# Two groups of gate products together ahead of every second score piece, instead of one ahead of each

## The chip, the cores and the metric

The kernel runs on one core of one Trainium2 chip, in one launch. The time is the device time of one execution in microseconds (us), the median of several executions. A profile is one further execution, recorded engine by engine: TensorE (PE, with its weight loads as PEld), VectorE (DVE), ScalarE (ACT), GpSimd (POOL) and SyncE (SP), which here issues the loads.

## The reference, cut to what matters

Two transformer blocks are computed one after the other on 256 tokens of width 1024. The change touches only the last layer of the second block, a feed-forward layer with 16384 experts (128 x 128), of which each of 8 heads picks 16 per token:

```python
def block(hb):                                   # 128 tokens at a time, TOK_BLOCK = 128
    q = (hb @ w_pq).reshape(TOK_BLOCK, PEER_HEADS, 2, PEER_DHALF)
    s = jnp.einsum('thpd,hpnd->thpn', q, sub_keys).astype(jnp.float32)
    s1, i1 = lax.top_k(s[:, :, 0], PEER_TOPK)
    s2, i2 = lax.top_k(s[:, :, 1], PEER_TOPK)
    ...                                          # idx, top_s: the best 16 of the 256 sums per head
    gate = jax.nn.softmax(top_s, axis=-1).astype(hb.dtype)
    u = expert_u[idx]
    act = jax.nn.gelu(jnp.einsum('thkd,td->thk', u, hb), approximate=False)
    vv = expert_v[idx]
    return jnp.einsum('thk,thkd->td', gate * act, vv)
```

Everything is float32.

## The kernel before, in words

The kernel does not gather experts. It computes the scores of all 16384 experts for all 256 tokens, puts gelu over them, multiplies by a gate that is zero where an expert was not chosen, and multiplies the result with all of `expert_v`. The experts come in 128 pieces of 128. The tile `GE` [128 partitions, 128 pieces, 256 tokens] holds the products of gate and gelu.

A weight piece (512 KB) is loaded by SP into one of 4 buffers `raw`, and is split for TensorE into a high part, which ACT writes (`high`, a copy into the fp32r tile `spl`), and a low part, which DVE writes (`low`, raw minus high, a subtraction of 128x1024). `spl` has 3 places (`NSP = 3`), so `high(i)` waits until TensorE has used piece i-3 (`w_used`). Each program does its part of the split three pieces ahead: `w.past("eu", c)` makes `high(c+3)` on ACT and `low(c+3)` on DVE.

The pieces of `expert_u` (`eu`) run in one loop over c = 0 to 127 that stands once in the program of each engine, in an order written out by hand:

- TensorE (`scores(c)`): 24 matmuls 128x256 in fp32r into one PSUM bank. From c = 47 on, for 64 pieces, `gates(g)` stands ahead of `scores(c)`: 8 matmuls 128x128 in fp16 for the four tokens of group g, from the operands `Ao` and `EB` into another bank. It waits for the one-hots of its group (`Ao`). 4 banks are in turn for both.
- ACT: `put(g)` copies that part of the gates whose pieces have no scores yet from PSUM into `GE`; it waits for DVE's `G_mul` of the same group. Then `scores(c)`: gelu over the bank of the scores, in two parts. Tokens whose gates are already in `GE` (columns 0 to n, n = `gated(c)`) go to the buffer `gl`, the others straight to `GE`. Then `high(c+3)`.
- DVE: `gate_scored(g)` multiplies the gates of group g onto the pieces already scored (a scalar_tensor_tensor that reads PSUM), then `onehots(c+2-GATES)` writes the operands of the group two ahead (two products into `EB`, two into `Ao`), then `gate_chunk(c-1)` multiplies `gl` onto the gates of piece c-1, then `low(c+3)`.
- `EB` and `Ao` have two buffers each (`g % 2`): `onehots(g)` waits until the products of group g-2 are done.

After piece 127 the stage of `expert_v` begins, in which TensorE accumulates the output over 128 pieces of 24 matmuls 128x512.

Below, c is a piece and g a group (before: g = c - 47). E(c) is the moment at which the 24 matmuls of `scores(c)` are issued and TensorE goes on to what stands behind them. All helpers record one line for an operation: L133 is every matmul, L155 every activation, L158 every tensor_tensor, L167 every scalar_tensor_tensor.

Of the kernel before, what the change touches and what calls it, by code (L numbers as in the profile page):

```python
# [23 lines left out]
         ("w_pq", 16, 1024, 1), ("sub_keys", 2, 1024, 0), ("eu", 128, 1024, 1), ("ev", 128, 1024, 1)]  # L24
ON_POOL = ("w_pq", "w_o", "w_xk", "w_xv", "w_rwkv_0", "w_rwkv_1")
EU_POOL, LOOKUP, WO_POOL = 30, 27, 3
CHOICE, GATES, NGRP = 42, 47, 64
PIECES = [(nm, j, n, sp) for nm, cnt, n, sp in ORDER for j in range(cnt)]
AT = {nm: i for i, (nm, j, _, _) in enumerate(PIECES) if j == 0}
SPLIT = [i for i, p in enumerate(PIECES) if p[3]]  # L30
# [186 lines left out]
def bc(ap, axis, n):  # L217
    u = ap.unsqueeze(axis)
    shape = list(u.shape)
    shape[axis] = n  # L220
    return u.to_broadcast(shape)
# [41 lines left out]
def build(nc, T, poff, outs, stop=99):  # L263
# [4 lines left out]
    with ctx:  # L268
# [187 lines left out]

        def gated(c):

            return 4 * min(max(c - GATES + 1, 0), NGRP)

        ge_at = SE.at
        GE = SE("GE", [128, 128, 256])
# [48 lines left out]
        def run(g):  # L511
            for _ in g:
                pass
# [10 lines left out]
        def tensor(pe):  # L524
# [741 lines left out]
            def scores(c):  # L1266
                wh, wl, i = weight("eu", c)
                b = pe.bank("eu", c)
                for k in range(8):
                    cs = slice(k * 128, k * 128 + 128)  # L1270
                    pe.wait_ge("xs_l", k)
                    last = pe.mm3(b[:, 0:256], (wh[:, cs], wl[:, cs]), tuple(t[:, k, :] for t in xT), k == 0, k == 7)
                last.then_inc("w_used", i)
                pe.give("eu", c, "ge", c)

            def gates(g):
                b = pe.bank("gates", g)
                pe.wait_ge("Ao", g)
                for q in range(4):
                    for k in range(2):  # L1280
                        last = pe.mm(b[:, q * 128:q * 128 + 128], EB[:, g % 2, 1, q // 2, :, q % 2], Ao[:, g % 2, k, q // 2, :, q % 2], k == 0, k == 1)
                last.then_inc("gates_ps", g)
                pe.give("gates", g, "G", g)
# [12 lines left out]

            ch = [choose(0), choose(1)]
            for c in range(128):
                if GATES <= c < GATES + NGRP:
                    gates(c - GATES)  # L1300
                scores(c)
                if c == CHOICE + 2:
                    run(ch[0])
                    run(ch[1])
# [21 lines left out]
        def scalar(act):  # L1326
# [374 lines left out]
            def choose(tb):  # L1701
                act.wait_ge("sel_sub", tb)
                act.wait_ge("x5_rs", tb)
                sg_ = sel[:, tb, 2, :].rearrange("p (h k) -> p h k", k=16)
                act.act(sg_, sg_, ACT.Exp, scale=s_x5[tb][1]).then_inc("sel_exp", tb)

            def scores(c):
                n = gated(c)
                if not n:
                    w.past("eu", c)  # L1710
                act.wait_ge("w_used", AT["eu"] + c)
                if n < 256:
                    x = act.act(GE[:, c, n:256], act.ps("eu", c)[:, n:256], ACT.Gelu)
                if n:
                    if c >= GATES + 2:
                        act.wait_ge("W_mul", c - 2)
                    x = act.act(gl[:, c % 2, 0:n], act.ps("eu", c)[:, 0:n], ACT.Gelu)
                x.then_inc("ge", c)
                w.past("eu", c)

            def put(g):

                s = GATES + g
                act.wait_ge("gate")
                act.wait_ge("sel_ps")
                act.wait_ge("G_mul", g)
                act.act(GE[:, s:128, 4 * g:4 * g + 4], act.ps("gates", g)[:, :].rearrange("p (t i) -> p i t", t=4)[:, s:128, :], ACT.Copy, scale=1.0 / GSCALE).then_inc("G", g)
# [5 lines left out]
                act.act(Wr[:, c % 2, 0, :], GE[:, c, :], ACT.Copy).then_inc("W_h", c)  # L1733

            for c in range(128):
                if GATES <= c < GATES + NGRP:
                    put(c - GATES)
                scores(c)
                if c == CHOICE:
                    for tb in range(2):  # L1740
                        choose(tb)
# [11 lines left out]
        def vector(dve):  # L1753
# [116 lines left out]
            for tb in range(2):  # L1870
# [3 lines left out]
                c, s = (bc(trig[:, i, tb, 0:8], 1, 16) for i in (1, 0))  # L1874
# [258 lines left out]
            def directions(j):  # L2133

                js = slice(2 * j, 2 * j + 2)
                z, y, x = be[:, js, :], y_[:, js, :], x2_[:, js, :]
                dve.wait_ge("P")
                dve.tt(ARt[:, js, 1, :], pm[:, js, :], Pc[:, js, :], ALU.mult).then_inc("rho", j)
                yield
                dve.wait_ge("y0", j)  # L2140
                v = dve.tt(z, y, y, ALU.mult).own()
                dve.wait_ge("Pi")
                dve.tt(aa[:, js, :], aa[:, js, :], cum[:, js, :], ALU.mult)
                yield
                dve.after(v)
                dve.after(dve.stt(z, z, -0.5, x, ALU.mult, ALU.mult).own())
                dve.after(dve.stt(y, z, 1.5, y, ALU.add, ALU.mult).own())
                yield
                dve.after(dve.tt(t1[:, js, :], t1[:, js, :], y, ALU.mult).then_inc("kk", j))
                dve.wait_ge("Pp")  # L2150
                dve.tt(ARt[:, js, 0, :], t1[:, js, :], ld[:, js, :], ALU.mult).then_inc("al", j)
                yield
                dve.tt(z, t1[:, js, :], aa[:, js, :], ALU.mult).then_inc("be", j)


            g = directions(0)
# [4 lines left out]
            g = directions(1)  # L2161
# [51 lines left out]
            for tb in range(2):  # L2213
                for i, (sc, half) in enumerate(((1, 0), (0, 1), (1, 1), (0, 0))):
                    g = rows[:, 2048:2240].rearrange("p (j d) -> p j d", j=2)[:, :, 64 + 16 * half:80 + 16 * half]
# [288 lines left out]
            def parted():  # L2504

                dve.wait_ge("slT")
                dve.after(dve.cp(gp[:, 0, :], sg[:, :]).own())
                return dve.tt(gp[:, 1, :], sg[:, :], gp[:, 0, :], ALU.subtract).own()

            def onehots(g):  # L2510
                if g >= 2:
                    dve.wait_ge("gates_ps", g - 2)
                ts = slice(4 * g, 4 * g + 4)
                eb, ao = EB[:, g % 2, :, :, :, :], Ao[:, g % 2, :, :, :, :]
                pair = lambda t, a: bc(t[:, :, 4 * g + 2 * a:4 * g + 2 * a + 2], 2, 128)
                made = [dve.tt(eb[:, :, a, :, :], bc(io2[:, :, :], 1, 2), pair(idx, a), ALU.is_equal).own() for a in range(2)]
                for a in range(2):
                    dve.after(made[a])
                    x = dve.tt(ao[:, :, a, :, :], bc(eb[:, 0, a, :, :], 1, 2), pair(gp, a), ALU.mult)
                x.then_inc("Ao", g)  # L2520

            def gate_scored(g):

                s = GATES + g
                dve.wait_ge("gates_ps", g)
                dve.wait_ge("ge", s - 1)
                o = GE[:, 0:s, 4 * g:4 * g + 4]
                dve.stt(o, dve.ps("gates", g)[:, :].rearrange("p (t i) -> p i t", t=4)[:, 0:s, :], 1.0 / GSCALE, o, ALU.mult, ALU.mult).then_inc("G_mul", g)

            def gate_chunk(c):  # L2530

                n = gated(c)
                dve.wait_ge("ge", c)
                dve.wait_ge("G", n // 4 - 1)
                dve.tt(GE[:, c, 0:n], GE[:, c, 0:n], gl[:, c % 2, 0:n], ALU.mult).then_inc("W_mul", c)
# [11 lines left out]
            for x in ch:  # L2547
                next(x)
            for c in range(128):
                if GATES <= c < GATES + NGRP:  # L2550
                    gate_scored(c - GATES)
                if GATES <= c + 2 < GATES + NGRP:
                    onehots(c + 2 - GATES)
                if c > GATES:
                    gate_chunk(c - 1)
                w.past("eu", c)
                if LOOKUP <= c < CHOICE:
                    next(lk, None)
                if c == CHOICE:
                    for x in ch:  # L2560
                        next(x)
                if c == CHOICE + 2:
                    for x in ch:
                        run(x)
                    dve.after(parted())
# [151 lines left out]

        marks = Marks(nc, ctx)
        lanes = [("pe", tensor), ("dve", vector), ("act", scalar), ("pool", gpsimd), ("sp", sync)]
        for name, program in lanes:  # L2720
            program(Lane(marks, name, ident, banks, {}))
# [11 lines left out]
        @block.tensor  # L2733
        def _(e):
            tensor(lane("pe", e))

        @block.vector
        def _(e):
            vector(lane("dve", e))

        @block.scalar
        def _(e):
            scalar(lane("act", e))
# [81 lines left out]
```

## Time and profile before

| | |
|---|---|
| median of 3 runs | 1484.4 us (1483.9 to 1486.01) |
| the profiled execution | 1486.74 us, its span 1484.7 us |
| granted TensorE clock, mean | 0.995 |
| PE busy | 1441.2 us, 97% of the span |
| DVE busy | 1006.8 us, 68% |
| ACT busy | 721.9 us, 49% |
| pieces with gate products | from 852.8 us to 1065.5 us |

Busy time is an average over stages. What a change inside one loop is worth is read in the time order of that loop: which instruction each engine waits for, and how late it is. Matmuls overlap, so their spacing is read from start to start. A row of the time order that is marked x2 or x24 joins so many instructions of a kind, from the start of the first to the end of the last.

### The profile page before, as it was taken

The page shows a single profiled execution, that of the slowest core. Times are in us where ns is not written, and L with a number is a line of the kernel's source. Part 1 is how long each engine was busy: PE and PEld are TensorE (multiplying, and loading weights), DVE is VectorE, ACT ScalarE, POOL GpSimd, SP SyncE. Part 2 cuts the span into 40 slices and gives each one's busy share as a digit, 9 for nine tenths or more (in the row PEclk, how much of TensorE's full clock was granted, in tenths as well). Part 3 has the DMA queues.
Part 4 walks back from the last instruction along what each step waited for, and adds up shares of the span by engine and source line. Part 5 has one row for each costly group of instructions (what it writes and reads, how often), then busy time and mean ns, then how long its engine had stood idle before and what let it go on. Part 6 is the DMA issues. An engine that isn't in the chain of part 4 may idle for free.

```text
span 1484.7 us, 24608 instructions
## 1 busy us (share of the span) xinstructions
PE 1441.2 (97%) x10160; PEld 1291.4 (87%) x10160; DVE 1006.8 (68%) x1809; ACT 721.9 (49%) x1195; POOL 239.1 (16%) x115
## 2 busy tenths in 40 slices
PE   7999999999998989999999999999999999999998
PEld 6898797998878968979999999999998888888886
DVE  5667465665449787663798788999855555555554
ACT  4565453555344635343544555544444444444443
POOL 0037000000014220539684000000000000000000
PEclk9999999999999999999999999999999999999999
DMA  7634443556552520135566655555565666666663
GB/s 276 217 104 142 144 141 113 157 182 191 190 175 86 167 68 2 45 114 166 175 185 187 182 159 158 156 158 157 162 187 168 190 186 186 190 189 186 186 191 118
DMA packets 64878, 235.23 MB, mean 158 GB/s; under 512 B 7424, under 2 KB 7680, under 8 KB 64512
## 3 DMA queue, kind: packets, MB, share of 16 engines
q1 hardware_dynamic: 63904, 231.60, 50.7%
q10 hardware_dynamic: 864, 2.08, 0.4%
q8 instruction: 80, 1.31, 0.4%
q14 instruction: 30, 0.25, 0.1%
HBM read 232.60 MB, written 1.05 MB: 157 GB/s over the span
## 4 chain that ended last, share of the span: by engine, by line
PE 87%; DVE 9%; ACT 2%; issue 1%; DMA 0%; POOL 0%; DVEq 0%; ACTq 0%; POOLq 0%
PE ps L133 85%; PE ps L142 1%; DVE spl L158 1%; DVE pm L167 1%; ACT QK L155 1%; DVE pm L158 1%; DVE prep L158 0%; DMA hA<-in_x 0%; ACT spl L155 0%; DVE hx L158 0%; DVE pR L158 0%; DVE junk L158 0%; DVE hx L161 0%; DVE be L158 0%; DVE ez L167 0%
## 5 line engine op out<-in xcount | busy, mean ns | idle before, releaser
L133 PE MATMUL ps<-xhl,spl 128*128 128x256 f32 x4944 | 605.8, 283 | 3.5 <-POOL spl L158 1.6
L133 PEld LDWEIGHTS ps<-xhl,spl 128*128 128x128 f32 x4944 | 591.0, 189 | 6.3 <-issue 3.3
L158 DVE TENSOR_TENSOR spl<-raw,spl 128x1024 fp32r<-128x1024 f32 (+2 forms) x356 | 430.3, 1214 | 236.2 <-ACT spl L155 234.6
L155 ACT ACTIVATE spl<-raw 128x1024 fp32r<-128x1024 f32 (+1 forms) x435 | 454.6, 1048 | 273.6 <-PE ps L133 259.0
L133 PE MATMUL ps<-spl,Wr 128*128 128x512 f32 x1536 | 358.7, 395 | 1.1 <-DVE Wr L158 1.1
L133 PEld LDWEIGHTS ps<-spl,Wr 128*128 128x128 f32 x1536 | 288.3, 188 | 71.3 <-DVE Wr L158 1.3
L158 POOL TENSOR_TENSOR spl<-raw,spl 128x1024 fp32r<-128x1024 f32 x79 | 199.8, 2543 | 275.8 <-ACT spl L155 275.3
L155 ACT ACTIVATE Wr<-GE 128x256 fp32r<-128x256 f32 x128 | 53.5, 419 | 183.5 <-PE ps L133 183.5
L158 DVE TENSOR_TENSOR Wr<-GE,Wr 128x256 fp32r<-128x256 f32 x128 | 54.3, 425 | 81.5 <-ACT Wr L155 81.5
L155 ACT ACTIVATE GE<-ps 128x256 f32<-128x256 f32 (+42 forms) x176 | 54.0, 326 | 113.6 <-DVE GE L167 108.4
L133 PE MATMUL ps<-spl,ahl 128*128 128x512 f32 x384 | 90.1, 396 | 0.0
L133 PEld LDWEIGHTS ps<-spl,ahl 128*128 128x128 f32 x384 | 72.2, 188 | 17.6
L133 PE MATMUL ps<-spl,yhl 128*128 128x512 f32 x288 | 69.4, 399 | 1.4 <-ACT vm L155 1.4
L133 PEld LDWEIGHTS ps<-spl,yhl 128*128 128x128 f32 x288 | 53.7, 188 | 14.3 <-ACT vm L155 1.6
L133 PE MATMUL ps<-spl,xhl 128*128 128x512 f32 (+2 forms) x288 | 62.5, 375 | 0.9 <-DVE spl L158 0.8
L133 PEld LDWEIGHTS ps<-spl,xhl 128*128 128x128 f32 x288 | 51.5, 190 | 11.0 <-DVE spl L158 2.0
L158 DVE TENSOR_TENSOR Ao<-EB,gp 128x512 f16<-128x512 f16 x128 | 48.2, 418 | 0.0
L158 DVE TENSOR_TENSOR EB<-io,idx 128x512 f16<-128x512 f16 x128 | 48.0, 417 | 0.0
L133 PE MATMUL ps<-Ao,EB 128*128 128x128 f16 x512 | 40.9, 221 | 0.0
L158 POOL TENSOR_TENSOR stats<-stats,neghalf 128x1 f32<-128x1 f32 (+2 forms) x13 | 8.0, 613 | 202.0 <-DVE stats L161 202.0
L155 ACT ACTIVATE gl<-ps 128x256 f32<-128x256 f32 (+32 forms) x81 | 24.1, 298 | 25.6 <-PE ps L133 25.6
L133 PEld LDWEIGHTS ps<-Ao,EB 128*128 128x128 f16 x512 | 29.7, 97 | 2.7
(341 smaller groups left out, 1156.3 us busy)
## 6 DMA issues: line engine op xcount, KB each, us to landing
raw<-in_eu SPq DMA_DIRECT2D x128, 512.0 KB, 3.6
raw<-in_ev SPq DMA_DIRECT2D x128, 512.0 KB, 4.3
raw<-in_w_up SPq DMA_DIRECT2D x32, 512.0 KB, 3.6
raw<-in_w_down SPq DMA_DIRECT2D x32, 512.0 KB, 4.3
raw<-in_w_in_a SPq DMA_DIRECT2D x16, 512.0 KB, 5.0
raw<-in_w_pq SPq DMA_DIRECT2D x16, 512.0 KB, 3.6
raw<-in_w_rwkv SPq DMA_DIRECT2D x14, 512.0 KB, 3.7
raw<-in_w_in_t SPq DMA_DIRECT2D x8, 512.0 KB, 3.5
```

The source lines that it names most:

```text
L133: return Done(self, self.e and self.e.matmul(out, l, r, start=st, stop=sp))
L142: return Done(self, self.e and self.e.transpose(out, in_, self.ident[0:n, 0:n]))
L155: return Done(self, self.e and self.e.activation(out, a, f, bias=bias, scale=scale, accum_out=acc))
L158: return Done(self, self.e and self.e.tensor_tensor(out, a, b, op))
L167: return Done(self, self.e and self.e.scalar_tensor_tensor(out, a, s, b, o0, o1))
```

## The change

The constant `GATES` goes from 47 to 48. A new helper `groups(c)` gives the groups of a piece: for an even distance from 48 the two groups c-48 and c-47, for an odd one none. TensorE makes both groups' products ahead of `scores(c)`, ACT puts both, DVE does both `gate_scored`, and both count as if they stood at the first piece of the pair. The one-hots stay where they were relative to `GATES`: one group at each piece, `onehots(c + 2 - GATES)`. The even groups thus come one piece later than before, the odd groups at the same piece as before, and all one-hots one piece later. `gated(c)` now goes up by 8 at every second piece. The buffers of `EB` and `Ao` stay at two.

```diff
-CHOICE, GATES, NGRP = 42, 47, 64
+CHOICE, GATES, NGRP = 42, 48, 64
...
         def gated(c):
 
-            return 4 * min(max(c - GATES + 1, 0), NGRP)
+            return 4 * min(max((c - GATES) // 2 * 2 + 2, 0), NGRP)
+
+        def groups(c):
+
+            return range(c - GATES, c - GATES + 2) if GATES <= c < GATES + NGRP and (c - GATES) % 2 == 0 else ()
...
             for c in range(128):
-                if GATES <= c < GATES + NGRP:
-                    gates(c - GATES)
+                for g in groups(c):
+                    gates(g)
                 scores(c)
...
             def put(g):
 
-                s = GATES + g
+                s = GATES + g // 2 * 2
...
-                if GATES <= c < GATES + NGRP:
-                    put(c - GATES)
+                for g in groups(c):
+                    put(g)
...
             def gate_scored(g):
 
-                s = GATES + g
+                s = GATES + g // 2 * 2
...
-                if GATES <= c < GATES + NGRP:
-                    gate_scored(c - GATES)
+                for g in groups(c):
+                    gate_scored(g)
                 if GATES <= c + 2 < GATES + NGRP:
                     onehots(c + 2 - GATES)
```

DVE's order at pieces 102 and 103, before. `GE<-ps,GE` is `gate_scored`, `EB` and `Ao` are the one-hots, `GE<-GE,gl` is `gate_chunk`, `spl<-raw,spl` is `low`; the brackets name the semaphores waited for.

```order
L167 SCALAR_TENSOR_TENSOR GE<-ps,GE 128x102x4 [waits ge,pe_ps]
L158 TENSOR_TENSOR EB<-io_121,idx 128x2x256 x2
L158 TENSOR_TENSOR Ao<-EB,gp 128x2x256 [waits own_dve] x2
L158 TENSOR_TENSOR GE<-GE,gl 128x220 [waits G]
L158 TENSOR_TENSOR spl<-raw,spl 128x1024 [waits w_high]
L167 SCALAR_TENSOR_TENSOR GE<-ps,GE 128x103x4 [waits ge,pe_ps]
L158 TENSOR_TENSOR EB<-io_121,idx 128x2x256 x2
L158 TENSOR_TENSOR Ao<-EB,gp 128x2x256 [waits own_dve] x2
L158 TENSOR_TENSOR GE<-GE,gl 128x224 [waits G]
L158 TENSOR_TENSOR spl<-raw,spl 128x1024 [waits w_high]
```

The same two pieces of DVE in the changed kernel.

```order
L167 SCALAR_TENSOR_TENSOR GE<-ps,GE 128x102x4 [waits ge,pe_ps]
L167 SCALAR_TENSOR_TENSOR GE<-ps,GE 128x102x4 [waits pe_ps]
L158 TENSOR_TENSOR EB<-io_121,idx 128x2x256 x2
L158 TENSOR_TENSOR Ao<-EB,gp 128x2x256 [waits own_dve] x2
L158 TENSOR_TENSOR GE<-GE,gl 128x216
L158 TENSOR_TENSOR spl<-raw,spl 128x1024 [waits w_high]
L158 TENSOR_TENSOR EB<-io_121,idx 128x2x256 x2
L158 TENSOR_TENSOR Ao<-EB,gp 128x2x256 [waits own_dve] x2
L158 TENSOR_TENSOR GE<-GE,gl 128x224 [waits G,ge]
L158 TENSOR_TENSOR spl<-raw,spl 128x1024 [waits w_high]
```

Both `gate_scored` stand at the even piece. The second one-hots stand behind the `low` of the even piece, and nothing but a `gate_chunk` and a `low` is left between them and the next pair.

TensorE's order where the gate products begin, in the changed kernel (`Ao,EB` are gate products, `xhl,spl` scores); before, 8 and 24 matmuls alternated.

```order
L133 MATMUL ps<-xhl,spl 128x256 x72
L133 MATMUL ps<-Ao,EB 128x128 x16
L133 MATMUL ps<-xhl,spl 128x256 x48
```

The products of both groups of a pair stand together. Those of the odd group, the last 8 of the 16, stand one `scores` piece behind DVE's one-hots of that group, where two pieces lay between them before; those of the even group still stand two pieces behind.

## Rows read from the trace of the kernel before

**Rows 1.** The page: the chain by engine; gate matmuls: busy us, mean ns | idle.

```profile
PE 87%; DVE 9%; ACT 2%; issue 1%; DMA 0%; POOL 0%; DVEq 0%; ACTq 0%; POOLq 0%
...
L133 PE MATMUL ps<-Ao,EB 128*128 128x128 f16 x512 | 40.9, 221 | 0.0
```

**Rows 2.** Stretch: length, busy PE PEld DVE ACT POOL, clock, DMA, GB/s.

```profile
1000.00:1050.00 50.00, 50.00 (x478) 49.38 (x477) 49.11 (x106) 24.09 (x60) 0.00 (x0) 1.00 0.53 154
```

**Rows 3.** The waits, 853 to 1065.5 us: who for whom, total, times, longest.

```profile
ACT GE L155 <- DVE GE L167: 106.6, 63, 2.0
DVE spl L158 <- ACT spl L155: 12.0, 39, 0.5
```

**Rows 4.** Order of time, pieces 102 and 103: start us, us, engine, line, out<-in.

```profile
1038.17 0.64 PE L133 MATMUL ps<-Ao,EB 128*128 128x128 f16 x8
...
1038.62 3.08 PE L133 MATMUL ps<-xhl,spl 128*128 128x256 f32 x24
...
1040.93 0.58 DVE L167 SCALAR_TENSOR_TENSOR GE<-ps,GE 128x408 f32<-128x408 f32 x1
1041.43 0.75 DVE L158 TENSOR_TENSOR EB<-io,idx 128x512 f16<-128x512 f16 x2
...
1041.54 0.64 PE L133 MATMUL ps<-Ao,EB 128*128 128x128 f16 x8
1041.55 0.39 ACT L155 ACTIVATE GE<-ps 128x104 f32<-128x104 f32 x2 [1.79 <-DVE GE L167]
...
1042.06 1.06 ACT L155 ACTIVATE spl<-raw 128x1024 fp32r<-128x1024 f32 x1
1042.10 0.75 DVE L158 TENSOR_TENSOR Ao<-EB,gp 128x512 f16<-128x512 f16 x2
1042.77 0.38 DVE L158 TENSOR_TENSOR GE<-GE,gl 128x220 f32<-128x220 f32 x1
1043.16 1.22 DVE L158 TENSOR_TENSOR spl<-raw,spl 128x1024 fp32r<-128x1024 f32 x1
1044.30 0.58 DVE L167 SCALAR_TENSOR_TENSOR GE<-ps,GE 128x412 f32<-128x412 f32 x1
```

**Rows 5.** Order of time of DVE, two score pieces without gate products.

```profile
822.14 1.23 DVE L158 TENSOR_TENSOR spl<-raw,spl 128x1024 fp32r<-128x1024 f32 x1 [0.48 <-ACT spl L155]
...
824.98 1.23 DVE L158 TENSOR_TENSOR spl<-raw,spl 128x1024 fp32r<-128x1024 f32 x1 [0.48 <-ACT spl L155]
```

**Rows 6.** Order of time, an early gate piece.

```profile
873.04 0.64 PE L133 MATMUL ps<-Ao,EB 128*128 128x128 f16 x8
...
874.65 1.23 DVE L158 TENSOR_TENSOR spl<-raw,spl 128x1024 fp32r<-128x1024 f32 x1 [0.42 <-ACT spl L155]
```

**Rows 7.** Order of time where the gate products begin.

```profile
852.35 1.22 DVE L158 TENSOR_TENSOR spl<-raw,spl 128x1024 fp32r<-128x1024 f32 x1
...
852.82 0.64 PE L133 MATMUL ps<-Ao,EB 128*128 128x128 f16 x8
853.07 1.06 ACT L155 ACTIVATE spl<-raw 128x1024 fp32r<-128x1024 f32 x1 [1.50 <-PE ps L133]
...
853.49 0.75 DVE L158 TENSOR_TENSOR EB<-io,idx 128x512 f16<-128x512 f16 x2
```

**Rows 8.** Order of time where TensorE waits for DVE, start of `expert_v`.

```profile
1119.81 0.42 DVE L158 TENSOR_TENSOR Wr<-GE,Wr 128x256 fp32r<-128x256 f32 x1
...
1120.29 0.50 PE L133 MATMUL ps<-spl,Wr 128*128 128x512 f32 x1 [1.12 <-DVE Wr L158]
```

**Rows 9.** The same in an earlier stage.

```profile
709.94 0.69 DVE L170 COPY qP<-ps 128x512 f32<-128x512 f32 x1 [10.66 <-PE ps L133]
...
710.77 0.46 PE L133 MATMUL ps<-raw,qP 128*128 128x128 f32 x2 [0.88 <-DVE qP L170]
```

**Rows 10.** Busy us per stretch, columns as in rows 2: two stretches in which TensorE waits.

```profile
460.00:480.00 20.00, 17.68 (x127) 15.42 (x126) 19.55 (x25) 6.64 (x10) 8.36 (x4) 1.00 0.23 74
...
522.00:524.00 2.00, 0.00 (x0) 0.00 (x0) 0.79 (x7) 0.00 (x0) 1.01 (x1) 0.50 0.74 180
```

## The prediction

> **What bounds the kernel now.** I read the page first: TensorE carries 87% of the chain that ended last [rows 1]. Then the busy time by stretch: with gate products, TensorE is busy for all of 50 us and DVE for 49.11 [rows 2]. A busy DVE is no bound as such, so I read the waits of that stretch: none is TensorE's. ACT waits for DVE's `gate_scored` (106.6 us over 63 pieces), and DVE's `low` for ACT's `high` (12.0 us) [rows 3]. So TensorE sets the pace and DVE has little left over. The order of time gives the rest [rows 4]:
>
> - TensorE's period is 1041.54 - 1038.17 = 3.37 us a piece: 0.45 from the first gate matmul to the first score matmul, 2.92 from there to the next gate matmul.
> - Score pieces without gates follow each other in 824.98 - 822.14 = 2.84 us [rows 5]. So 0.08 of the 2.92 is paid once at each change from gate matmuls to score matmuls. One gate matmul lasts 0.22 [rows 1] and eight together 0.64, so they start (0.64 - 0.22) / 7 = 0.06 apart, and a second group behind a first costs 8 x 0.06 = 0.48.
> - `low` of piece c+3 starts 1043.16 - 1041.54 = 1.62 us after E(c) (here c = 102), late in the stage, and 874.65 - 873.04 = 1.61 early in it [rows 4, 6]. Without gates at all the `low` follows `high` in the same way [rows 5]. This distance is gelu, then `high` (1042.06 + 1.06 = 1043.12), then a handoff of 0.04. It cannot be shorter, since `high(c+3)` writes into the place that `scores(c)` has just read.
>
> **The change part by part.**
>
> *Matmuls.* None are added. Of 64 changes from gates to scores 32 go: a pair of groups costs 0.48 + 0.45 + 0.08 = 1.01 where two single groups cost 2 x (0.45 + 0.08) = 1.06. That is -0.05 x 32 = -1.6 us, if nothing waits.
>
> *DVE and ACT work.* The counts stay: 64 `gate_scored`, 64 one-hots, 64 `put`. Half the `gate_scored` read one piece more, half the chunks are 4 columns shorter. I cost it at nothing: two neighbouring `gate_scored` differ by no more than 0.01 us (0.58 and 0.58, [rows 4]), and DVE is about to wait longer than that in each pair.
>
> *The one-hots.* This is the term that decides. For a pair at even piece e, TensorE runs gates(g), gates(g+1), scores(e), scores(e+1), then gates(g+2), gates(g+3). DVE runs two `gate_scored`, onehots(g+2), chunk(e-1), **low(e+3), onehots(g+3)**, chunk(e), low(e+4). The one-hots of the odd group are queued behind low(e+3), which waits for `high(e+3)`, which waits for the end of scores(e). Before, the same order cost nothing, since the one-hots written there were wanted two pieces on; now gates(g+3) is wanted one piece after. Counted from E(e):
>
> - When TensorE wants gates(g+3): scores(e+1) takes 2.84, gates(g+2) 0.48, so E(e) + 3.32.
> - When its `Ao` is there: low(e+3) starts at +1.62 [rows 4, 6]. From `low` to the next DVE start it is 1044.30 - 1043.16 = 1.14 [rows 4], and to an `EB` as well (853.49 - 852.35 = 1.14, [rows 7]). From the first `EB` to the end of the second `Ao` it is 1042.10 + 0.75 - 1041.43 = 1.42 [rows 4]. Sum: +4.18.
> - The handoff from DVE to TensorE: 1120.29 - 1120.23 = 0.06 in one place [rows 8], 710.77 - 710.63 = 0.14 in another [rows 9], and 0.04 from DVE to ACT (1041.51 to 1041.55, [rows 4]). I take 0.06, the one of a tensor_tensor whose result TensorE reads, and keep 0.04 and 0.14 for the range. So gates(g+3) starts at +4.24.
> - The stall is 4.24 - 3.32 = 0.92 us.
>
> The period of a pair is then 4.24 up to gates(g+3), and from its start 0.45 + 0.08 + 2.84 = 3.37 to E(e+2): 7.61 us, against 2 x 3.37 = 6.74. That is +0.87 a pair, at every pair alike, since no term in it depends on c.
>
> What is queued behind, and is it late next? Behind onehots(g+3) on DVE stand chunk(e) and low(e+4). The latter may start at E(e+1) + 1.62 = E(e) + 4.46 and does start at about 1.62 + 1.14 + 1.34 + 0.39 = 4.49 (1.34 from `EB` to chunk, 0.39 from chunk to low, [rows 4]); scores(e+4) wants it only in the pair after the next. Then come `low` 1.14, two `gate_scored` of up to 0.50 each (1041.43 - 1040.93), one-hots 1.34 and a chunk 0.39: DVE is free for low(e+5) at +8.36, and that may start at 7.61 + 1.62 = 9.23. So DVE waits 0.87 in each pair even late in the stage and is not the bound. The second `put` can start at 4.49 + 1.14 + 1.00 + 0.04 = 6.67 and has two activations of 0.39 together before it is in the way of the gelu of E(e+2) = +7.61. gates(g+2) needs its bank free from put(g), long past. SP's loads hang on `low`, which is no more than 0.03 later against TensorE than before.
>
> *First pair.* E(46) = 852.82 [rows 7]; now nothing stands between scores(46) and scores(47), so E(47) = 855.66 and gates(1) is wanted at 856.14. high(49) ends at 854.13 [rows 7], low(49) starts at 854.17 and `Ao` of group 1 is done 2.56 later at 856.73; with the handoff 856.79. This stall is 0.65.
>
> *Sum.* 31 stalls of 0.92 and one of 0.65 are 29.2; less 1.6 for the changes saved: +27.6 us. Against the profiled execution (1486.74, span 1484.7) that is 1514.3; the median of the runs lies 2.3 below the profiled one, so the forecast for the median is 1484.4 + 27.6 = 1512.0 us, 1.9% slower. Nothing gives it back: the `expert_v` stage is TensorE at its own pace.
>
> *A rule of the clock.* TensorE waits for 0.92 of every 7.61 us. In this trace waits that add up to 2.32 of 20 us leave the granted clock at 1.00, its level of 2.4 GHz, and after a long wait it is 0.50, the level of 1.2 GHz [rows 10]. The Trainium skill, "TensorE: Matmul & The Clock Gate", section "A second HAM failure mode: psum-queue depth-cycling", tells of a kernel in which frequent short idles between groups of matmuls made the clock swing between the two levels. Its result is the rival C below; rows 10 speak against it.
>
> **The rivals.**
>
> A. *The one-hots are in time, and only the saved changes show.* This is the case on the other side. It decides at E(e) + 3.32: `Ao` would have to be done 0.92 us sooner, so low(e+3) would have to start at +0.70, not +1.62. For it speaks only that DVE's waits are few now (12.0 us in 39 pieces, [rows 3]). Against it stand 1.62 and 1.61, measured late and early, and the wait of `low` written in the order. The time would be 1484.4 - 1.6 = 1482.8.
>
> B. *A second wait joins.* For instance the matmul behind the wait cannot load its weights ahead, or the `put` of two groups holds up the gelu and with it `high`. The first is at most one weight load a pair; if the handoff is also 0.14, the two add 0.08 + 0.10 and give 27.6 + 32 x 0.18 = +33.4, the top of my forecast. A held gelu would add what it is held for; its slack is 7.61 + 0.2 - 6.67 - 0.4 = 0.7 at the least. If this were all used up and 0.3 a pair beyond, it would be 1512.0 + 9.6 = 1521.6.
>
> C. *The clock.* Were TensorE granted the lower level for all pairs, the score matmuls of each, 2 x 2.84, would take twice as long, 5.68 more, up to 182 us in all; a tenth of that gives 1530.
>
> D. *Half the stall.* In the trace before, ACT's `put` of the same piece begins at the very moment of E(c) (1041.55 against 1041.54, [rows 4]) and so stands ahead of the gelu. After the change both `put` are over by then, and the gelu could begin sooner. Were the 1.62 shorter by a `put`, about 0.4 at the most, since two activations last 0.39, the stall would be 0.5: 1484.4 + 32 x 0.5 - 1.6 = 1498.8. Against it: early in the stage, where a `put` is about three times as wide, `low` comes at the same 1.61 [rows 6], so the gelu seems to wait for TensorE and not for the `put`.
>
> **How the numbers follow.** The forecast 0.87, A 0.03, B beyond the forecast 0.04, C 0.02, D 0.04. The forecast's bounds: below, handoff 0.04 and a `low` 0.06 sooner (the margin I allow on a distance read as 1.61 and 1.62) take 32 x 0.08 = 2.6 off, 1509.4; above, 1484.4 + 33.4 = 1517.8. The range 1507 to 1518 leaves out A, C, most of B and D. A measurement of this kernel tells 0.2% from no change, 3 us. Faster or the same is only A, whose 1482.8 lies within 0.2%: 0.02 for the same, 0.01 for faster. Slower 0.97.
>
> **What would show it.** In the profile after: waits of TensorE for DVE's `Ao`, 32 of them, 0.9 us each, some 29 us in all, which is a row that is not there now; gate matmuls x16 broken into 8 and 8 with the gap between them; a pair every 7.6 us, early and late alike; `low` of the even piece still 1.6 us behind E(e); DVE waiting about 0.9 to 1.5 us a pair for ACT's `spl`; busy TensorE time about unchanged, the `expert_v` stage unchanged and only shifted. A pair period of 6.7 us and no such row would make the prediction wrong; so would a period that grows along the stage (DVE bound), or a granted clock below 1.00 in it.

## The result, and the profile after

| | before | after |
|---|---|---|
| median | 1484.98 us (4 runs) | 1515.60 us (4 runs, 1514.48 to 1517.67) |
| ratio after / before | | 1.0208, 95% interval 1.019 to 1.0226 |
| profiled execution, its span | 1486.74, 1484.7 us | 1516.39, 1514.4 us |
| PE, DVE, ACT busy | 1441.2, 1006.8, 721.9 us | 1442.7, 1006.6, 723.7 us |
| granted clock, mean | 0.995 | 0.997 |

The changed kernel is slower by 30.6 us; the forecast was +27.6 us (1512.0 us, range 1507 to 1518). The forecast started from 1484.4 us, the median before as it then stood; with one more run it is 1484.98. No engine has more to do. What is new is a wait. First the row of the gate matmuls on the page of the kernel after (busy us, mean ns | idle of the engine ahead of them, and what ended it), which answers to the second of [rows 1]:

```profile
L133 PE MATMUL ps<-Ao,EB 128*128 128x128 f16 x512 | 40.5, 220 | 27.2 <-DVE Ao L158 27.2
```

The waits from 853 to 1100 us of the kernel after, against [rows 3] (who for whom, total us, times, longest):

```profile
ACT GE L155 <- PE ps L133: 77.2, 62, 1.4
ACT GE L155 <- DVE GE L167: 56.1, 42, 1.8
DVE spl L158 <- ACT spl L155: 44.5, 39, 2.2
PEld ps L133 <- issue: 31.9, 32, 1.0
PE ps L133 <- DVE Ao L158: 27.2, 32, 0.9
```

TensorE, which waited for nobody here before, waits 32 times for DVE's `Ao`, once in each pair. DVE itself waits more for ACT's `high` than before: up to 1096 us, where the gate products end, it is 42.3 us in 38 waits, against 12.0 us in 39 before (the 44.5 above take in one wait behind the gate products). It is held up, not overloaded. The row `PEld ps L133 <- issue` is the same 32 places, seen at TensorE's weight loads. ACT, which before waited for DVE 106.6 us, now waits for TensorE most.

The busy time of the late gate pieces, columns as in [rows 2]:

```profile
1000.00:1050.00 50.00, 44.01 (x417) 42.67 (x417) 42.94 (x92) 21.63 (x51) 0.00 (x0) 1.00 0.43 137
```

TensorE was busy for all of such a stretch before and now for 44.01 us, DVE for 49.11 before and now for 42.94. All engines do less in the same time, since they go through one loop; that alone does not say which step holds them up. The clock stays at 1.00, from 855 to 1096 us too.

The order of time of one late pair of the kernel after (start us, us, engine, line, out<-in), against [rows 4]. The first gelu is the row at 1036.83, `high(e+3)` the one at 1037.16, `low(e+3)` the one at 1038.25, the one-hots of the odd group are the `EB` at 1039.39 and the `Ao` at 1040.06:

```profile
1033.27 0.62 PE L133 MATMUL ps<-Ao,EB 128*128 128x128 f16 x8 [0.86 <-DVE Ao L158]
...
1033.70 5.92 PE L133 MATMUL ps<-xhl,spl 128*128 128x256 f32 x48
...
1036.83 0.23 ACT L155 ACTIVATE GE<-ps 128x64 f32<-128x64 f32 x1 [0.97 <-PE ps L133]
...
1037.16 1.06 ACT L155 ACTIVATE spl<-raw 128x1024 fp32r<-128x1024 f32 x1
1038.25 1.22 DVE L158 TENSOR_TENSOR spl<-raw,spl 128x1024 fp32r<-128x1024 f32 x1 [1.12 <-ACT spl L155]
1039.39 0.75 DVE L158 TENSOR_TENSOR EB<-io,idx 128x512 f16<-128x512 f16 x2
...
1039.47 0.64 PE L133 MATMUL ps<-Ao,EB 128*128 128x128 f16 x8
...
1040.06 0.75 DVE L158 TENSOR_TENSOR Ao<-EB,gp 128x512 f16<-128x512 f16 x2
...
1040.96 0.62 PE L133 MATMUL ps<-Ao,EB 128*128 128x128 f16 x8 [0.85 <-DVE Ao L158]
```

Read it backwards from 1040.96. The matmul follows the end of `Ao` (1040.06 + 0.75 = 1040.81). `EB` and `Ao` follow `low` without a wait (rows of DVE overlap a little, so 1.14 from start to start is the pace). `low` follows `high` (1037.16 + 1.06 = 1038.22), after DVE had waited 1.12 us. `high` follows the gelu, and the gelu follows E(e), where the first 24 of the 48 score matmuls are issued: the second 24 take 2.84, so E(e) = 1039.47 - 2.84 = 1036.63. The gelu starts 0.20 behind it, after ACT had waited 0.97 for TensorE, and `low` stands 1.62 behind it, as before the change. From 1033.27 to 1040.96 it is 7.69 us, against 2 x 3.37 before. The two groups of a pair begin 1.49 apart (1039.47, 1040.96), where 0.48 would do: each pair is held up by 1.01 us. The row gives the wait as 0.85, since it counts idle only from the modelled end of the matmul before.

Early in the stage it is the same, 910.16 - 902.47 = 7.69:

```profile
902.47 0.63 PE L133 MATMUL ps<-Ao,EB 128*128 128x128 f16 x8 [0.86 <-DVE Ao L158]
...
910.16 0.62 PE L133 MATMUL ps<-Ao,EB 128*128 128x128 f16 x8 [0.85 <-DVE Ao L158]
```

The `expert_v` stage is only shifted, by 1149.97 - 1120.29 = 29.68 us ([rows 8] and this row of the kernel after):

```profile
1149.97 0.73 PE L133 MATMUL ps<-spl,Wr 128*128 128x512 f32 x2 [1.12 <-DVE Wr L158]
```

### The profile page after: what moved, and what is told of

It is laid out like the page before. It is cut to its first block, busy times and chain, and to the rows that moved or that the text cites. A ratio compares the mean times of both kernels' runs of the same rounds, so it can differ in the third digit from the quotient of the medians.

```text
span 1514.4 us, 24607 instructions
## 1 busy us (share of the span) xinstructions
PE 1442.7 (95%) x10160; PEld 1289.3 (85%) x10160; DVE 1006.6 (66%) x1808; ACT 723.7 (48%) x1194; POOL 239.2 (16%) x115
## 4 chain that ended last, share of the span: by engine, by line
PE 77%; DVE 14%; ACT 5%; issue 2%; DMA 1%; POOL 0%; ACTq 0%; DVEq 0%; POOLq 0%
PE ps L133 76%; DVE spl L158 4%; ACT spl L155 3%; DVE EB L158 1%; DVE Ao L158 1%; PE ps L142 1%; DVE pm L167 1%; DMA raw<-in_w_in_a 1%; ACT GE L155 1%; ACT QK L155 1%; DMA par<-in_par 1%; DVE pm L158 0%; DVE prep L158 0%; DVE hx L158 0%; DVE pR L158 0%
## 5 line engine op out<-in xcount | busy, mean ns | idle before, releaser
L133 PE MATMUL ps<-xhl,spl 128*128 128x256 f32 x4944 | 598.0, 282 | 3.7 <-POOL spl L158 1.7
L133 PEld LDWEIGHTS ps<-xhl,spl 128*128 128x128 f32 x4944 | 589.0, 188 | 6.7 <-issue 3.8
L133 PE MATMUL ps<-spl,Wr 128*128 128x512 f32 x1536 | 358.7, 395 | 1.1 <-DVE Wr L158 1.1
L133 PEld LDWEIGHTS ps<-spl,Wr 128*128 128x128 f32 x1536 | 288.2, 188 | 71.3 <-DVE Wr L158 1.3
L155 ACT ACTIVATE GE<-ps 128x256 f32<-128x256 f32 (+34 forms) x176 | 56.4, 326 | 139.2 <-PE ps L133 82.3
L133 PE MATMUL ps<-spl,ahl 128*128 128x512 f32 x384 | 90.1, 396 | 0.0
L133 PEld LDWEIGHTS ps<-spl,ahl 128*128 128x128 f32 x384 | 72.2, 188 | 17.6
L133 PE MATMUL ps<-spl,yhl 128*128 128x512 f32 x288 | 69.4, 399 | 1.4 <-ACT vm L155 1.4
L133 PE MATMUL ps<-Ao,EB 128*128 128x128 f16 x512 | 40.5, 220 | 27.2 <-DVE Ao L158 27.2
L133 PEld LDWEIGHTS ps<-spl,yhl 128*128 128x128 f32 x288 | 53.7, 188 | 14.3 <-ACT vm L155 1.6
L133 PE MATMUL ps<-spl,xhl 128*128 128x512 f32 (+2 forms) x288 | 62.4, 374 | 1.6 <-DVE spl L158 1.5
L133 PEld LDWEIGHTS ps<-spl,xhl 128*128 128x128 f32 x288 | 51.3, 189 | 11.9 <-DVE spl L158 3.1
L133 PEld LDWEIGHTS ps<-Ao,EB 128*128 128x128 f16 x512 | 30.1, 97 | 33.2 <-issue 31.9
L155 ACT ACTIVATE gl<-ps 128x256 f32<-128x256 f32 (+31 forms) x80 | 23.8, 297 | 26.5 <-PE ps L133 26.5
```

The source lines that it names most:

```text
L133: return Done(self, self.e and self.e.matmul(out, l, r, start=st, stop=sp))
L155: return Done(self, self.e and self.e.activation(out, a, f, bias=bias, scale=scale, accum_out=acc))
```

## The experiments

Times are medians; each ratio is against the kernel before on the same chip, with its 95% interval. All but the second start from the changed kernel. Its 1515.6 us was measured beside a kernel before of 1484.98 us, a loss of 30.6; the kernel before took 1485.45 us beside the first four experiments and 1485.92 us beside the last two, so a loss against that is the fairer comparison and is given too.

### Both one-hots ahead of `low(e+3)`

```diff
-                if GATES <= c + 2 < GATES + NGRP:
-                    onehots(c + 2 - GATES)
+                for g in groups(c + 2):
+                    onehots(g)
```

> The changed kernel with one edit: DVE writes the one-hots of both groups of the next pair at the even piece, ahead of low(e+3), and none at the odd piece. Theory (the stall is the one-hots of the odd group queued behind low(e+3)): the 32 waits of TensorE for Ao go, all of the 30 us come back, and the 32 saved changes from gate to score matmuls show: 1483 to 1485 us, a pair every 6.69 us of TensorE. Rival (pairing as such costs, by banks or by the put of two groups): TensorE still waits in each pair, 1500 us or more. What could spoil it late in the stage: DVE's own work of a pair is about 6.7 us, as much as TensorE's, so a few tenths of a us may be lost in the last pairs.

Measured: 1482.63 us (12 runs; before on the same chip 1485.45, 23 runs), ratio 0.9983, interval 0.9971 to 0.9995: 0.4 us under the expected 1483 to 1485. TensorE has no wait for `Ao` left. Two pairs of this kernel, PE alone and DVE's `low`:

```profile
1035.24 1.10 PE L133 MATMUL ps<-Ao,EB 128*128 128x128 f16 x16
1035.26 1.22 DVE L158 TENSOR_TENSOR spl<-raw,spl 128x1024 fp32r<-128x1024 f32 x1
...
1036.15 5.91 PE L133 MATMUL ps<-xhl,spl 128*128 128x256 f32 x48
...
1041.90 1.10 PE L133 MATMUL ps<-Ao,EB 128*128 128x128 f16 x16
```

The 16 gate matmuls stand in one row without a gap, and a pair takes 1041.90 - 1035.24 = 6.66 us. Pairs of 6.66 and 6.68 alternate, so on average a pair is 0.07 shorter than the 6.74 before. So the pairing is not what costs, and neither are the banks nor the two `put`; where the one-hots of the odd group stand is all of the loss. What the pairing is worth by itself is small: 2.8 us, by the interval 0.7 to 4.3, of which the shorter pairs make 32 x 0.07 = 2.2.

`low(e+3)` now comes later, at 1035.26 where E(e) is 1035.24 - 2.84 = 1032.40, so 2.86 behind it instead of 1.62, without any harm: scores(e+3) wants it only in the next pair. What has room to be late was put behind what has none.

### The shift of the start alone

```diff
-CHOICE, GATES, NGRP = 42, 47, 64
+CHOICE, GATES, NGRP = 42, 48, 64
```

This is the kernel before with this one edit.

> The kernel before with GATES = 48 and nothing else: one group ahead of each piece, all of it one piece later. Theory: the shift costs nothing, 1484 to 1486 us, no wait of TensorE for Ao. Rival (the shift is part of the loss, since the gates end one piece later): some us slower than before.

Measured: 1485.02 us (12 runs), ratio 0.9998, interval 0.9987 to 1.0009. The period stays 1003.40 to 1006.77, 3.37 us:

```profile
1003.40 0.64 PE L133 MATMUL ps<-Ao,EB 128*128 128x128 f16 x8
1003.85 3.08 PE L133 MATMUL ps<-xhl,spl 128*128 128x256 f32 x24
1006.77 0.64 PE L133 MATMUL ps<-Ao,EB 128*128 128x128 f16 x8
```

Beginning one piece later is free.

### One more DVE instruction, behind `low` or ahead of it

A product of the kind of an `EB`, into a tile `scr` that nobody reads, once in a pair, at the odd piece ahead of the one-hots or at the even piece behind the chunk. These are two kernels; the cut shows both places, with a comment for which kernel each is:

```diff
+        scr = SO("scr", [128, 2, 128, 2], F16)
...
+            last_extra = []
+
+            def extra(g):
+                dve.after(*last_extra)
+                last_extra[:] = [dve.tt(scr[:, :, :, :], bc(io2[:, :, :], 1, 2), bc(idx[:, :, 4 * g:4 * g + 2], 2, 128), ALU.is_equal).own()]
...
+                if GATES <= c + 2 < GATES + NGRP and (c - GATES) % 2:      # first kernel: behind low(e+3)
+                    extra(c + 2 - GATES)
                 if GATES <= c + 2 < GATES + NGRP:
                     onehots(c + 2 - GATES)
                 if c > GATES:
                     gate_chunk(c - 1)
+                if GATES <= c + 3 < GATES + NGRP and (c - GATES) % 2 == 0: # second kernel: ahead of low(e+3)
+                    extra(c + 3 - GATES)
```

> The changed kernel with one more DVE instruction in each pair (an EB product of 128x512 into a tile that nobody reads, 0.33 us from start to start), between low(e+3) and the one-hots of the odd group. Theory (low, one-hots, handoff, gates, scores are one closed chain): each pair grows by 0.33 us, 32 x 0.33 = 10.7 us over the changed kernel: 1526 us, TensorE waits 1.19 us a pair. Rival (DVE has time to spare in each pair, 1.1 us of idle before low, which takes it up): no change, 1515.6.

> The same additional DVE instruction, the same number of times, but ahead of low(e+3), behind the chunk of the even piece. Theory: there DVE waits about 1.1 us for high(e+3) anyway, so it costs nothing: 1515 to 1516 us. Rival (the pair is bound by the sum of DVE's work): 1526 us, as with the instruction at the other place.

Measured behind `low`: 1526.68 us (4 runs), ratio 1.0275, interval 1.0253 to 1.0297, 11.1 above the changed kernel's 1515.6 (10.7 expected); against the kernel before on the same chip the loss is 41.2, so 10.6 more than 30.6. Ahead of `low`: 1516.80 us (4 runs), ratio 1.0206, interval 1.0184 to 1.0227, as good as the changed kernel's 1.0208 (a loss of 31.4 against 30.6). The order of time of the kernel with it behind `low`:

```profile
1029.94 1.23 DVE L158 TENSOR_TENSOR spl<-raw,spl 128x1024 fp32r<-128x1024 f32 x1 [1.29 <-ACT spl L155]
1031.08 0.42 DVE L158 TENSOR_TENSOR scr<-io,idx 128x512 f16<-128x512 f16 x1
...
1031.42 0.75 DVE L158 TENSOR_TENSOR EB<-io,idx 128x512 f16<-128x512 f16 x2
...
1032.99 0.63 PE L133 MATMUL ps<-Ao,EB 128*128 128x128 f16 x8 [1.19 <-DVE Ao L158]
```

And of the kernel with it ahead:

```profile
1031.05 0.42 DVE L158 TENSOR_TENSOR scr<-io,idx 128x512 f16<-128x512 f16 x1
...
1032.28 1.23 DVE L158 TENSOR_TENSOR spl<-raw,spl 128x1024 fp32r<-128x1024 f32 x1 [0.81 <-ACT spl L155]
...
1035.00 0.63 PE L133 MATMUL ps<-Ao,EB 128*128 128x128 f16 x8 [0.86 <-DVE Ao L158]
```

The same instruction, the same number of times: behind `low` it takes TensorE's wait from 0.85 to 1.19, 0.34 more, as long as `scr` takes from its start to that of `EB`. Ahead of `low` it comes out of DVE's own wait, 1.15 in the same pair of the changed kernel and 0.81 here, and TensorE's wait stays. DVE's time counts in full behind `low` and not at all ahead of it, as long as DVE waits there. The rival of a DVE that is the bound by its sum is out.

### `high` ahead of the gelu on ACT

```diff
                 act.wait_ge("w_used", AT["eu"] + c)
+                if groups(c):
+                    w.past("eu", c)
                 if n < 256:
```

> The changed kernel with ACT's order at the even pieces turned round: high(e+3) ahead of the two gelu of scores(e), instead of behind them. Both wait for the same end of scores(e). Theory: low(e+3) and all behind it come 0.33 us sooner (the time from the first gelu's start to high's start), so a pair takes 7.36 us instead of 7.69: 32 x 0.33 = 10.6 us less than the changed kernel, 1505 us. Rival (the gelu is needed as early as it is, by the chunk or the bank of the next scores): the gain is given back, 1515 us or more.

Measured: 1506.12 us (4 runs), ratio 1.0125, interval 1.0101 to 1.0149; 9.5 below the changed kernel's 1515.6, and 10.6 was expected; against the kernel before on the same chip the loss is 20.2, so 10.4 less than 30.6. `high` now begins 0.2 behind E(e), with the gelu behind it; the start of `low` moves from 1.62 to 1024.89 - (1026.44 - 2.84) = 1.29 behind E(e), and TensorE's wait falls from 0.85 to 0.53. A pair takes 7.36 us, as expected:

```profile
1023.80 1.06 ACT L155 ACTIVATE spl<-raw 128x1024 fp32r<-128x1024 f32 x1 [0.67 <-PE ps L133]
...
1024.77 0.21 ACT L155 ACTIVATE GE<-ps 128x72 f32<-128x72 f32 x1
...
1024.89 1.23 DVE L158 TENSOR_TENSOR spl<-raw,spl 128x1024 fp32r<-128x1024 f32 x1 [0.49 <-ACT spl L155]
...
1026.44 0.64 PE L133 MATMUL ps<-Ao,EB 128*128 128x128 f16 x8
...
1027.61 0.63 PE L133 MATMUL ps<-Ao,EB 128*128 128x128 f16 x8 [0.53 <-DVE Ao L158]
```

So the chain does run through ACT, as the prediction's 1.62 has it, and 0.33 of the 1.62 is only ACT's order, the gelu ahead of `high`.

### One semaphore less at the second group

```diff
             def gates(g):
-                b = pe.bank("gates", g)
+                b = pe.ps("gates", g)
...
+                for g in groups(c):
+                    pe.bank("gates", g)
                 for g in groups(c):
                     gates(g)
```

`pe.bank` waits for the semaphore by which the bank is free (`G`, set by `put`). Here both banks are waited for ahead of the first group, so the first matmul of the second group waits for `Ao` alone. The bank had been free for long at that point, before and after this edit.

> The changed kernel in which TensorE waits for the PSUM banks of both groups ahead of the first, so that the first matmul of the second group waits for one semaphore (Ao) instead of two (Ao and the bank's G). In the trace the handoff from the end of Ao to the matmul took 0.147 us at all 32 places, against 0.055 where the expert_v stage waits for one semaphore. Theory: the second semaphore costs the 0.09, so 32 x 0.09 = 2.9 us go: 1512.7 us, handoff 0.055. Rival (the longer handoff belongs to the operand, fp16 or moving, not to the wait): 0.147 and 1515.6 stay.

Measured: 1513.14 us (4 runs), ratio 1.017, interval 1.0147 to 1.0192; 2.5 below the changed kernel's 1515.6, and by the loss against the kernel before on the same chip (27.2 against 30.6) 3.4 below, with 2.9 expected. The intervals of the two ratios overlap, so the median alone does not show it. The trace does. The kernel with one semaphore:

```profile
1026.10 0.75 DVE L158 TENSOR_TENSOR Ao<-EB,gp 128x512 f16<-128x512 f16 x2
...
1026.91 0.65 PE L133 MATMUL ps<-Ao,EB 128*128 128x128 f16 x8 [0.77 <-DVE Ao L158]
...
1034.53 0.64 PE L133 MATMUL ps<-Ao,EB 128*128 128x128 f16 x8 [0.77 <-DVE Ao L158]
```

`Ao` ends at 1026.85 and the matmul starts 0.06 later, where with two semaphores it was 1040.81 to 1040.96, 0.15. At all 32 places the start is 0.056 to 0.057 behind `Ao` here and 0.146 to 0.147 in the changed kernel. The pair takes 1034.53 - 1026.91 = 7.62 instead of 7.69. The rival, that the longer handoff belongs to the operand, is out: operands and matmuls are the same. What differs on TensorE's side is told in the last section.

## Why the prediction was right, point by point

- *Where it hurts.* Right. `low(e+3)` and the one-hots of the odd group behind it hold up gates(g+3) in each pair, 32 waits, early and late alike. Moving these one-hots alone brings everything back (1482.63).
- *`low` at +1.62, `low` to `EB` 1.14, `EB` to the end of `Ao` 1.42.* Right: 1.62, 1039.39 - 1038.25 = 1.14, 1040.81 - 1039.39 = 1.42. But the sentence "It cannot be shorter" on the 1.62 is wrong. E(e) bounds the start of `high`, not the gelu that stands ahead of it: with `high` first, `low` starts at +1.29 and 10.4 us come back.
- *gates(g+3) wanted at +3.32.* Right: 2.84 and then 0.48; in the kernel with both one-hots in front 16 matmuls stand in a row.
- *The handoff from DVE to TensorE.* This is the mis-sized term. I took 0.06, the one of [rows 8], "the one of a tensor_tensor whose result TensorE reads". The kind of the DVE instruction made no difference here, 0.145 behind the copy of [rows 9] and 0.146 to 0.147 behind this tensor_tensor; what did was that two semaphores are waited for ahead of the matmul. Measured 0.147, so the stall is 1.01 and not 0.92, the pair 7.69 and not 7.61. 32 x 0.087 = 2.8 us are nearly all of the 3.0 between +27.6 and +30.6. The 0.14 of [rows 9] was the right row: there too the matmul stands behind the waits for more than one semaphore (`raw`, `qP_a`, `qP_v`). The range had been drawn to take in 0.14.
- *First pair.* Forecast 0.65. Measured: its groups begin 1.23 apart in the trace (855.09 and 856.31), less 0.48 is 0.75, the same 0.09 more.
- *DVE is not the bound.* Right: its wait for `high(e+3)` falls from 1.76 us early (the `low` at 861.29) over 1.12 to 0.94 in the last pair (1092.11), where 0.87 was the forecast and the longer handoff adds 0.09. The "0.9 to 1.5" of the signs was too low for the early pairs. An additional instruction ahead of `low` costs nothing.
- *The saved changes.* I gave 1.6 us. The kernel without the stall is 2.8 us faster than before on the same chip, with 0.7 to 4.3 by its interval, and its pair is 0.07 shorter than two single pieces, where I had 0.05, so 1.6 was fair and perhaps a little low.
- *The rivals.* A (one-hots in time) did not happen, but its time, 1482.8, is what the kernel with the moved one-hots gives. B's first part did by half: the longer handoff came, and no further 0.10 for a weight load. C: the granted clock is 1.00 in the stretch with a wait in each pair, 2.4 GHz, so the swing between the two levels did not occur, of which the Trainium skill tells for another kernel ("TensorE: Matmul & The Clock Gate", section "A second HAM failure mode: psum-queue depth-cycling"). D (a `put` hidden in the 1.62): `low` stays at 1.62 although both `put` are long over. The gelu starts 0.20 behind E(e) after ACT has waited 0.97 for TensorE, so no `put` was in its way.

How the sum closes: 31 x (7.69 - 7.61) and 0.1 for the first pair are 2.6; 27.6 + 2.6 = 30.2 for the stage. The `expert_v` stage starts 29.68 later in the trace and the span is 29.7 longer. The gate products began 0.57 earlier than the trace before would put them (855.09 against 852.82 + 2.84 = 855.66), a difference from stages that the change doesn't touch. So from the first gate products on it is 29.68 + 0.57 = 30.25, which is the sum.

## What to carry to other kernels

When work is bunched on one engine, look at what prepares it on the others: two products together need two operands together, and the second preparation must move with it, or it falls behind whatever waits stand in between in that engine's order. A low share of waits tells nothing of it; write down for each consumer how late its producer may be, and put the instruction that waits long but is wanted late (here `low(e+3)`) behind the one that is wanted soon. That all engines get slower together does not tell where the loop is held up; a small instruction put inside or outside it, at the same count, tells whether a place lies on it.

## What the runs showed of the hardware that was not expected

A matmul that waits for a semaphore of DVE started 0.055 to 0.057 us after the DVE instruction's end where it waits for that one alone ([rows 8]; 32 places in the kernel with one semaphore less), and 0.146 to 0.147 us where a second semaphore is waited for at the same point (32 places in the changed kernel), although the second had long been reached.

The trace also records TensorE's semaphore instructions, which the rows shown here leave out, and they tell the two cases apart. With two semaphores the wait for `Ao` stands in a semaphore instruction of its own (from 1040.855 us, 0.051 long), and the first weight load of the group, which carries the wait for the bank, starts behind it at 1040.931. With one semaphore that weight load waits for `Ao` itself and starts at 1026.903, 0.05 behind `Ao`'s end. So the 0.09 us goes with this one additional instruction and not with every further semaphore: the matmul of [rows 9] stands behind three, two of them in one such instruction, and starts 0.145 behind the copy's end. Whether the 0.09 would go if `Ao` were on the weight load and the bank in the instruction ahead, no run here shows.

It costs time only where TensorE truly waits: the kernel with both one-hots in front has the same instruction ahead of its second groups (at 1035.10 us for the group that follows at 1035.66), and its 16 matmuls follow each other without a gap.
